# Two feed-forward networks and half of the queries and keys with the weights as the stationary operand, and ScalarE's root table loaded ahead of the norms

## The reference

```python
def hybrid_layer(x, ...):                       # two of them
    h = rms_norm(x, norm1_g)
    mq, mk, mv, mo, mi, mf, aq, ak, av = split(h @ w_in)
    qk = silu(centred_depthwise_conv(concatenate([mq, mk]), conv_w))   # 5 taps along the tokens
    ...                                         # mLSTM in both directions, dilated attention
    x = x + concatenate([y_m, y_a]) @ w_out
    u = relu(rms_norm(x, norm2_g) @ w_up)       # 1024 -> 4096
    return x + (u * u) @ w_down                 # 4096 -> 1024

def layer_norm(x, g, b):
    mu = mean(x); var = mean(square(x - mu))
    return (x - mu) * rsqrt(var + 1e-5) * g + b

# in the sparse attention
kc = silu(blk @ w1) @ w2                        # compressed keys; values alike
gates = sigmoid(g_logits)                       # 16 heads x 3 branches
```

## Time and profile before

| | us |
|---|---|
| median of 3 runs | 2278.53 (2272.89 to 2286.32) |
| the profiled execution | 2274.16 |
| its span, first to last instruction | 2272.4 |
| PE busy | 2145.5 (94%) |
| DVE busy | 1596.6 (70%) |
| ACT busy | 1324.1 (58%) |

### The profile page before, as it was taken

One profiled execution on the slowest core, in us unless ns is written; L12 is line 12 of the kernel. 1 busy time (PEld: TensorE's weight loads), 2 busy tenths in 40 slices (PEclk: granted clock), 3 DMA queues, 4 the chain that ended last, 5 costly groups with the idle time before them and its releaser, 6 DMA issues.

```text
span 2272.4 us, 26136 instructions
## 1 busy us (share of the span) xinstructions
PE 2145.5 (94%) x10090; PEld 1727.6 (76%) x10090; DVE 1596.6 (70%) x1554; ACT 1324.1 (58%) x1378; POOL 20.4 (1%) x32
## 2 busy tenths in 40 slices
PE   8889999989999999998888999999999999999997
PEld 7667887767788788777667888788888877777675
DVE  4965555776555645566755555788888899999997
ACT  5454444645444443445644544576776788887886
POOL 0000000000000000000000000000000000000000
PEclk9989999999999999997899999999999999999998
DMA  7314553431655455432007555788998999999995
GB/s 263 139 47 153 185 185 131 167 121 68 250 183 183 150 185 185 164 138 75 1 19 272 211 207 183 272 341 348 342 363 331 367 362 421 392 421 375 421 389 217
DMA packets 74625, 524.29 MB, mean 231 GB/s; under 512 B 8736, under 2 KB 9184, under 8 KB 12160
## 3 DMA queue, kind: packets, MB, share of 16 engines
q1 hardware_dynamic: 71712, 511.64, 59.2%
q0 software_dynamic: 2784, 10.93, 1.4%
HBM read 521.48 MB, written 1.05 MB: 230 GB/s over the span
## 4 chain that ended last, share of the span: by engine, by line
PE 66%; DVE 19%; ACT 6%; issue 6%; DMA 3%; DVEq 0%; ACTq 0%; SPq 0%; POOLq 0%
PE psum L516 57%; DVE LO L507 10%; ACT HI L499 2%; DMA ring<-in_experts 2%; DVE AR L1556 1%; PE psum L1030 1%; PE psum L2406 1%; PE psum L1025 1%; ACT AR L845 1%; PE psum L2434 1%; PE psum L879 1%; PE psum L816 1%; PE psum L664 1%; PE psum L683 1%; PE psum L1943 1%
## 5 line engine op out<-in xcount | busy, mean ns | idle before, releaser
L507 DVE TENSOR_TENSOR LO<-ring,HI 128x2048 fp32r<-128x2048 f32 x379 | 850.8, 2259 | 398.9 <-ACT HI L499 393.2
L499 ACT ACTIVATE HI<-ring 128x2048 fp32r<-128x2048 f32 x379 | 712.7, 1887 | 350.8 <-PE psum L516 340.3
L516 PE MATMUL psum<-HI,XT 128*128 128x512 f32 (+1 forms) x3152 | 805.2, 394 | 22.4 <-issue 5.7
L516 PEld LDWEIGHTS psum<-HI,XT 128*128 128x128 f32 x3152 | 592.4, 191 | 165.4 <-DVE XT L699 10.9
L516 PE MATMUL psum<-LO,XT 128*128 128x512 f32 (+1 forms) x1856 | 507.2, 395 | 16.6 <-DVE LO L507 14.2
L516 PEld LDWEIGHTS psum<-LO,XT 128*128 128x128 f32 x1856 | 345.4, 190 | 112.5 <-DVE LO L507 44.3
L516 PE MATMUL psum<-HI,HTH 128*128 128x512 f32 x848 | 306.3, 402 | 6.9 <-DVE HTH L1082 6.9
L507 DVE TENSOR_TENSOR LO<-AR,HI 128x2048 fp32r<-128x2048 f32 x112 | 254.9, 2290 | 53.6 <-ACT HI L499 53.0
L499 ACT ACTIVATE HI<-AR 128x2048 fp32r<-128x2048 f32 x112 | 212.7, 1911 | 60.3 <-PE psum L516 57.2
L516 PE MATMUL psum<-LO,HTH 128*128 128x512 f32 x848 | 229.9, 393 | 0.0
L516 PE MATMUL psum<-HI,HTL 128*128 128x512 f32 x568 | 221.5, 390 | 0.0
(11 more groups left out here) (270 smaller groups left out, 1464.8 us busy)
## 6 DMA issues: line engine op xcount, KB each, us to landing
ring<-in_experts SPq DMA_DIRECT2D x224, 1024.0 KB, 6.6
ring<-in_dense SPq DMA_DIRECT2D x149, 1024.0 KB, 4.8
AR<-in_experts SPq DMA_DIRECT2D x112, 1024.0 KB, 6.5
bcs<-in_ln_g POOLq DMA_DIRECT2D x4, 512.0 KB, 4.6
bcs<-in_ln_b POOLq DMA_DIRECT2D x4, 512.0 KB, 5.1
bcs<-in_norm_g POOLq DMA_DIRECT2D x3, 512.0 KB, 3.9
cons<-in_cons POOLq DMA_DIRECT2D x1, 1317.0 KB, 8.0
X<-in_x SPq DMA_DIRECT2D x2, 512.0 KB, 4.0
```

What stands on the lines that cost most here:

```text
L499: e.activation(HI[:, h:h + m], slot(u), ACT.Copy).then_inc(*high.up(u))
L507: e.tensor_tensor(LO[:, h:h + m], slot(u), HI[:, h:h + m].bitcast(F32), ALU.subtract).then_inc(*low.up(u))
L516: ins = e.matmul(out_ap, lhsT=a, rhs=b, start=start and n == 0, stop=stop and n == len(pairs) - 1)
```

## The change

1. A new helper `across`: a 128x128 tile of the weights is stationary and both token tiles stream as 256 columns. The output has the weights' columns in its partitions, so no transposes are needed. It is used for the keys (`raw`, part 1) in both hybrid layers and for the chunks c = 1 to 7 of `ff0` and `ff1` (`still`).
2. For those chunks `net_turn_tensor` returns at once; ScalarE and VectorE make HTH and HTL out of GS in SBUF. For the keys ScalarE empties the banks straight into `pad` (`pad_across`).
3. `first_root` is a square root of one column that nobody reads. It stands ahead of everything on ScalarE and ahead of the squares of tile 0 in l1, l2 and l3.
4. In layer 0 ScalarE squares tile 1 ahead of its copies of tile 0, TensorE turns tile 1 ahead of the first projection, and there are 3 and 6 idle matmuls where there were 10, 18 and 4.
5. In the sparse attention sigmoid and SiLU become Exp on ScalarE and, on VectorE, one more, a reciprocal and (SiLU) a product.

```diff
+        def across(e, use, key, x_ready):
+            for b in range(2):
+                banks.take(e, *use, b)
...
+            for i, u in enumerate(us):
...
+                e.wait_ge(*high.of(u))
+                for b in range(2):
+                    for j in range(2):
+                        products(e, banks.get(*use, b)[:, j * S:j * S + S],
+                                 [(hv[:, k, tile(b * 2 + j)], z[:, i * n + k, :]) for k in range(n)
+                                  for z in (XTH, XTL)], i == 0 and j == 0, False)
+                e.wait_ge(*low.of(u))
+                for b in range(2):
+                    for j in range(2):
+                        ins = products(e, banks.get(*use, b)[:, j * S:j * S + S],
+                                       [(lv[:, k, tile(b * 2 + j)], XTH[:, i * n + k, :])
+                                        for k in range(n)], False, last and j == 1)
...
+        def first_root(e):
+            e.wait_ge(*v_done.of("eps"))
+            e.wait_ge(*a_order.last)
+            e.activation(sm(1, "root"), EPS[:, 0:1], ACT.Sqrt).then_inc(*a_done.up())
...
         def ln_stat(e, name, t):
             ss, mv, r = sm(2, "ss", t), sm(2, "mv", t), sm(1, "r", t)
+            if t == 0 and name != "l0":
+                first_root(e)
...
+        def still(c, gated):
+            return c >= 1 and not gated
+
         def net_up_tensor(e, use, key, c, kinds, gated, ready, swap, tile1=None):
+            if still(c, gated):
+                return across(e, (use, "up", c), (key, "up", c), ready)
...
+            if still(c, gated):
+                for b in range(2):
+                    e.wait_ge(*v_done.of(use, "gate", c, b))
...
+                    e.activation(HTH[:, hb, 2 * b:2 * b + 2, :],
+                                 GS[:, hb, b, :].rearrange("p (j s) -> p j s", j=2),
+                                 ACT.Copy).then_inc(*a_done.up(use, "turn", c, b))
+                return between()
...
             if l == 0:
-                idle_first(e, 10)
+                idle_first(e, 3)
             turn_rows(e, n1, 0, lambda k: ROWS[:, 0, tile(k)], rows_of(n1, 0), rest=l)
-            if l == 0:
-                idle_first(e, 18)
...
-            cols_by_tile(e, ("raw", l, 0), ("qk", l, 0), BOTH, xr, between=second_rows)
-            cols(e, ("raw", l, 1), ("qk", l, 1), BOTH, xr)
+            if l == 0:
+                idle_first(e, 6)
+                second_rows()
+            cols_by_tile(e, ("raw", l, 0), ("qk", l, 0), BOTH, xr, between=second_rows if l else None)
+            across(e, ("raw", l, 1), ("qk", l, 1), xr)
             few(e, ("gates", l), ("gates", l), xr)
-            pad_tensor(e, l, 0)
+            pad_tensor(e, l)
...
-            pad_tensor(e, l, 1)
...
+        def pad_across(e, l):
+            for b in range(2):
+                e.wait_ge(*filled.of("raw", l, 1, b))
...
+                e.activation(pad[:, 4 + 2 * b:6 + 2 * b, 2:2 + S],
+                             banks.get("raw", l, 1, b).rearrange("p (b s) -> p b s", b=2),
+                             ACT.Copy).then_inc(*a_bank.up("raw", l, 1, b))
...
-                             ACT.Sigmoid).then_inc(*(a_bank.up("gates", 2, "turned") if t
+                             ACT.Exp, scale=-1.0).then_inc(*(a_bank.up("gates", 2, "turned") if t
...
-                e.activation(hv, hv, ACT.Silu).then_inc(*a_done.up("hid", kind))
+                e.activation(sm(60, "hid").rearrange("p (g n) -> p g n", g=4), hv, ACT.Exp,
+                             scale=-1.0).then_inc(*a_done.up("hid", kind))
...
+        def one_over_one_more(e, x):
...
+            e.tensor_scalar(x, x, 1.0, None, ALU.add).then_inc(*v_done.up())
...
+            e.reciprocal(x, x).then_inc(*v_done.up())
```

More of the change, by code:

```diff
@@ L985, in net_up_scalar @@
                 if c >= 2:
-                    e.wait_ge(*filled.of(use, "turn", c - 2, len(kinds) - 1))
+                    if still(c - 2, gated):
+                        e.wait_ge(*v_done.of(use, "turn", c - 2, t))
+                    else:
+                        e.wait_ge(*filled.of(use, "turn", c - 2, len(kinds) - 1))
                 e.wait_ge(*a_order.last)
@@ L1083, in net_turn_vector, with net_down_tensor @@
                                 ALU.subtract).then_inc(*v_done.up(use, "low", c, t))
-        def net_down_tensor(e, use, key, c, last, acc, kinds):
-            ready = [(v_bank if kind == P else v_done).of(use, "turn" if kind == P else "low", c, t)
-                     for t, kind in enumerate(kinds)]
+        def net_down_tensor(e, use, key, c, last, acc, kinds, gated):
+            ready = [(v_done if still(c, gated) or kind != P else v_bank).of(
+                use, "turn" if kind == P else "low", c, t) for t, kind in enumerate(kinds)]
             n = 0
@@ L2305, in sparse_vector, with gates @@
                 e.memset(buffer, 0.0).then_inc(*v_done.up())
+            def gates():
+                e.wait_ge(*a_bank.of("gates", 2, "turned"))
+                one_over_one_more(e, A(16000, 96))
             def keys_step():
```

130 lines of the change are left out of this document (94 added, 36 removed).

## The result

| | kernel before | changed kernel |
|---|---|---|
| median of the runs of this comparison | 2277.51 us (7 runs, 2269.47 to 2286.32) | 2264.29 us (7 runs, 2258.2 to 2269.45) |
| ratio to before | 1 | 0.9939, 95% interval 0.9918 to 0.9959 |
| the profiled execution, and its span | 2274.16 us, 2272.4 us | 2261.26 us, 2259.5 us |

The forecast was a median of 2266 us, from a gain of 12.65 us on the profiled execution. The median is 2264.29, and the profiled spans are 12.9 us apart. Timed once more later (run `e11_again`), the changed kernel gave 2263.35 us and a ratio of 0.9932 (0.9913 to 0.9951).

A forecast was written before the change was run, and what follows sets the result against it. TensorE was busy 94% of the span and held 66% of the chain. Terms of -4.8, +0.6, -2.1, -3.45 and -2.9 sum to -12.65 us: profiled 2274.16 becomes 2261.5, median 2278.53 becomes 2266; range 2255 to 2277 us.

The forecast's parts named there:

- Start: Layer 0 up to VectorE's gates: fewer idle matmuls and the new order save 4.8 us, between 2.5 and 6.5.
- Keys: Second half of queries and keys: gates 0.6 us later in layer 1; in layer 0 a vanished 0.7 us wait pays.
- Networks: ff0 and ff1: 14 chunks without transposes, 0.15 us less each after switches between widths, -2.1 us; ends -10 and +5.
- Rival C: 256-column matmuls run at the gate projection's 0.115 us, a chunk gives 0.7 us: -20 us, 2258; chance 0.14.
- Rival B: All 1536 matmuls of 256 columns bound by weight loads, 0.15 us each: +33 us, 2312; chance 0.06.
- Roots: Norms l1, l2, l3: table load moved ahead of the squares saves 1.15 us each, -3.45 us; ends -2.3 and -3.9.
- Sparse attention: Five table loads go, VectorE gets eight instructions: -2.9 us; ends -1 (SiLU's wait ends last at compressed keys) and -5.
- step on n = 4: Sparse attention: the weights of n = 4 start at 1057.75 instead of 1058.67, -0.9 us.
- step on n = 10: Sparse attention, second time: the weights of n = 10 start at 1079.15 instead of 1081.09, -1.9 us.
- Experts: From about 1200 us: the change does nothing there; forecast wrong if they begin less than 7 us earlier.
- A: Gains shrink to the loads: start 2.5, chunks nothing, the rest 5.75; -8 us, 2270; chance 0.25.
- D: A load issued ahead waits behind an eviction, stays on the path: at most 1.15 us a norm; 0.55 together with forecast.

The follow-up runs named there:

- e11_again: The changed kernel once more, no edit: 2263.35 us, ratio 0.9932.
- e2_start: Changed kernel with the start as before (ten idle matmuls first, squares and transposes in the old order): 2269.3 us, ratio 0.9948.
- e10_noidle: Changed kernel without any idle matmul at the start (3 and 6 in it): 2268.28 us, ratio 0.9951.
- e5_keys: Changed kernel with the second half of queries and keys as before (512 columns, transposes of part 1): 2259.67 us, ratio 0.991.
- e6_narrow: Changed kernel with each 256-column matmul of the networks and the second half of queries and keys cut into two of 128: 2421.35 us, ratio 1.0621.
- e4_roots: Changed kernel without the root issued ahead in l1, l2 and l3: 2264.7 us, ratio 0.9941.
- e3_tables: Changed kernel with Sigmoid and Silu and their five table loads back in the sparse attention, without VectorE's eight instructions: 2268.03 us, ratio 0.9957.
- e8_warm: Changed kernel with idle 512-column matmuls put into TensorE's gaps before sparse-key transposes and in the dilated attentions: 2275.38 us, ratio 0.9991.

## Why the prediction was right

**Start: -4.8 forecast, -4.63 and -4.60 measured** (gates; `e2_start`). The number is right by two errors that cancel. The norm vector landed at 8.4 us, not at 7.6 (in the other profiles between 7.5 and 8.6), so transposes (8.6 forecast, 9.26 measured) and the end of tile 0 and 1 (19.5 and 25.0 forecast, 26.1 measured for tile 1) came 0.7 to 1.1 us late. In return the slow beginning for which 0.7 us were kept did not come: the nine idle matmuls prevented it (`e10_noidle`).

**Keys: +0.6 in layer 1, measured +0.52**, by `e5_keys` 0.54. That the order of the start alone takes the wait in layer 0 away was right too (`e5_keys`).

**Networks: -2.1 forecast, -3.73 measured.** The term was mis-sized. The pace of 0.120 us and the 0.88 us of transposes were right, which gives -0.26 a chunk; I then kept 0.11 a chunk for the switches between widths, and there is none (0.23 us from the first matmul on). 14 times 0.265 is 3.7. Rival C, the pace of the gate row, did not happen. Rival B, the load that no longer lies under the matmul, needs 0.128 us a matmul; it is 0.120, and 0.112 where the columns are halved (`e6_narrow`). The Trainium skill's 81 ns at 128 columns ("TensorE: Matmul & The Clock Gate", section "Back-to-back issue gap") is not reached for this data.

**Roots: -3.45 forecast, -2.97 measured**, and 2.9 by `e4_roots`, of which some 0.4 is the clock, so about 2.5. The 1.15 us at VectorE were right in all three norms. The step that they pass on whole in `l1` and `l2` was wrong: "no other work beside them" leaves out TensorE, which is still at the matmuls of the stage before, so that only its own wait ahead of the transposes can be won, 0.85 and 0.54 us. In `l3`, at the end of the program, all of the 1.14 arrives. By the drain of 1.38 us beside a load that the Trainium skill states ("ScalarE: Activation LUTs", section "What ACT_TABLE_LOAD costs") it would have been 8 us; the runs contradict that.

**Sparse attention: -2.9 forecast, -2.54 measured**, the same in `e3_tables`. The step on n = 4 failed: it does not come 0.9 us earlier against the stage, but 0.35 later (6.75 against 7.10), because TensorE waits at the compressed keys for VectorE's SiLU, whose cost I had counted on VectorE alone. The range had this wait as its end of -1; only n = 4 met it. The step on n = 10 gave 2.2 where 1.9 was forecast.

**Experts: 7.2 to 8.1 us earlier**, where under 7 would have been wrong. What the forecast left out is the granted clock. In unchanged code three stages gave back 1.5 to 2.9 us; where I looked closer it was TensorE at half pace (24 matmuls of the output projection in 7.37 us, 5.80 before; 16 of the attention of layer 1 in 3.31, 1.79 before, both from the chain of waits). Medians over many executions even that out, single profiles do not; the sum over all such stages was -0.43 us, by luck.

So the total is right in part by luck: by the landmarks the networks gave 1.6 us more than forecast, the roots 0.5, the sparse attention 0.4 and the start 0.2 us less.

Of the other rivals, A (gains shrink, 2270) is refuted by the start and the chunk period. D, that a load issued ahead stays on the path, is refuted by the rows of `l1`.

## What to carry to other kernels

Turning a product around to save transposes pays only if the matmul stays wide enough to cover its weight load (here down to 256 columns), and only where TensorE is the bound: the same edit gave 3.7 us in the networks and cost 1.15 in front of VectorE's chain. A table load is worth moving where the row behind it waits for it. What it gives is its length less the next wait, and no more than the engine after that was waiting; look for such loads ahead of copies that TensorE waits for, too. When executions scatter by more than the effect of an edit, compare landmarks of an in-order engine stage by stage, and profile the same kernel twice before explaining a stage that was not edited.

## What the runs showed of the hardware

- A matmul of fp32r data with a 128x128 stationary tile took 0.112 us at 62 and at 128 columns, 0.120 at 256 and 0.227 at 512. Repeating the tile made no difference (5.75 us a unit either way).
- A matmul of plain 4-byte data took 0.86 us at 512 columns and full clock (`e8_warm`).
- The reciprocal on VectorE took 0.25 us at 16 columns, 0.53 at 60 and 0.75 at 96: it grows with columns faster than the add beside it (0.19 and 0.21 us at 60 and 96).
- Behind nine small idle matmuls and sixteen transposes the first eight matmuls took 2.09 us; without the idle ones 3.35 us.
- The granted clock fell to 0.50 for 24 us and for 44 us in the same stage of one kernel in two executions. Twelve small matmuls in TensorE's gaps ahead of it did not stop that (37.5 us); twelve of 0.86 us each kept it at 1.00 through that place, and it fell 23 us later for 10 us.
